# Half a turn later: low halves, value evictions and the norms of queries and keys in a two-block transformer kernel

## The chip, the cores and the metric

The kernel runs on one core of a Trainium2 chip. The metric is the device time of one execution in microseconds (us). Engines: PE is TensorE (matmuls; PEld its weight loads), DVE is VectorE, ACT is ScalarE, POOL is GpSimd, SP issues DMAs. Each engine works through its own queue in order and waits on semaphores of the others.

## The reference, cut to what matters

A sequence of 512 tokens with 1024 features goes through a first block and then two layers of a second one, all in float32. The first block has MoBA attention (8 heads of 64, queries and keys normed by head, a T5 bias), gated linear attention and a feed-forward part. Each of the two later layers has FoX attention (8 heads of 64, causal, a forget bias), retention (4 heads of 128) and a feed-forward part.

```python
mq = rms_norm(mq.reshape(B, S, MOBA_HEADS, MOBA_HEAD_DIM), moba_q_norm_g[layer])
mk = rms_norm(mk.reshape(B, S, MOBA_HEADS, MOBA_HEAD_DIM), moba_k_norm_g[layer])
...
p = softmax(q @ k.T * scale + bias)   # per head, causal
out = p @ v
```

The first two lines are the reference's; the last two sum up what both attentions compute (with 512 keys, MoBA's selected blocks are all past ones).

## The kernel before, in words

**Products.** Activations lie transposed (features on partitions, 512 tokens in a row). Every float32 product is made of three fp32r matmuls, high x high, high x low and low x high (`product`, L263 to L271); the same with the roles changed is `gemm_tok` (L335 to L340). So each operand needs a high half (a copy on ACT) and a low half (a subtraction on DVE). `prepare` (L239, L240) makes them for a weight piece of 128x1024, three pieces ahead; `piece` calls it at the start of a product of eight `product` steps. A product's PSUM bank (banks 0 to 3 in turn) is evicted by a function that is given to `gemm`: to `val` for MoBA's queries and keys (L712), to `gqk` (L521), and for FoX's rotary tiles by four DVE operations (L1346 to L1353).

**Ticks.** After each `product` the program calls `tick()`. A tick runs what `after_ticks(n, f)` has due, and then, by `pace[0]` steps per tick, steps of the background generator. This all happens when the instructions are issued to the queues: it fixes the order in each engine's queue, not a time. The attention heads are such a generator, `softmax_heads`, at 0.42 steps per tick in MoBA and 0.46 in FoX. A tick is some 0.69 us of PE work.

**Heads.** The generator goes through 32 turns (8 heads of 4 query blocks). Turn n has two steps. The first queues the reciprocal of turn n+2 (DVE, L635), the normalising of turn n+1 (ACT, L640), the scores of turn n+3 (PE, L616 and L618) and their bias, maximum and copy to SBUF (DVE, L621). The second queues, when n is a multiple of four, the weighing of the head that is complete (`weigh`, PE, L662, eight matmuls into bank 7) with its eviction, then the Exp of turn n+3 (ACT, L630), the transposes of turn n (PE, L647, into bank 6), and their high half (ACT, L652) and low half (DVE, L653). The transposes of the next turn wait until both halves have read bank 6. The weighing waits for the halves of all four turns. The eviction (`both_halves`, L698 on ACT, L699 on DVE) adds the two halves of the value product; for odd FoX heads a `split` into the operand Q follows (L399 on ACT, L400 on DVE).

**Norms of MoBA's queries and keys.** The evicted tile `val` waits nine ticks; then `qk_norm` (L580 to L597) queues at once: Square (ACT, L584), the mean over each head as a matmul with the constant `blk` into bank 7 (PE, L585), Ln (L586) and Exp (L588) on ACT, the gain on DVE (L591), and the splits of `queries` (L556, L557) or `keys` (L571, L572, with two copies by DMA each on POOL's queue). There are eight tiles, m = 0 to 7. The first two are evicted together, so their norms are due at the same tick. `rms_scale` and the gated linear attention use tB and other banks of their own.

Of the kernel before, what the change touches and what calls it, by code (L numbers as in the profile page):

```python
# [7 lines left out]
F32 = mybir.dt.float32  # L8
# [3 lines left out]
ALU = mybir.AluOpType  # L12
ACT = mybir.ActivationFunctionType
# [80 lines left out]
def build(nc, xT, w_in, gate_up, w_bm, w_bg, w_out, w_up, w_down, w_in2, w_out2, w_ff1, w_ff2,  # L94
          consts, params, out, vrev, cneg):
    ctx = ExitStack()
    with ctx:
        base = -(-nc.sbuf_base // 64) * 64

        def at(name, off_kb, shape, dt=F32):  # L100
            return nc.alloc_sbuf_tensor_at(name, shape, dt, offset=base + int(off_kb * KB))

        def sem(name):
            return Sem(ctx.enter_context(nc.semaphore(name)))

        PE, V, A, G, SP = (Queue(sem(n)) for n in ("s_pe", "s_dve", "s_act", "s_pool", "s_sp"))
# [24 lines left out]
        ident, blk = cst[:, 0:128], cst[:, 128:256]  # L131
# [4 lines left out]
        banks = [ctx.enter_context(nc.psum_tensor(f"ps{i}", [128, 512], F32)) for i in range(8)]  # L136
        free = [None] * 8
# [224 lines left out]
        def after_ticks(n, f):  # L362
            pending.append([n, f])
# [72 lines left out]
        sq = [at("sq0", g0 + 80, [128, S]), at("sq1", g0 + 82, [128, S])]  # L436

        sq_free, rb_free = [None, None], [None]
# [16 lines left out]
        t_const = [c9, t_prm, t_cst]  # L455
# [24 lines left out]
        val = [at(f"val{i}", g0 + 14 + 2 * i, [128, S]) for i in range(2)]  # L480
# [97 lines left out]

        val_free = [None, None]

        def qk_norm(heads, m, t_in):

            j, v, s = m // 2, val[m % 2], sq[m % 2]
            t = A.op(lambda e: e.activation(s[:, :], v[:, :], ACT.Square), t_in, sq_free[m % 2])  # L584
            t = PE.op(lambda e: e.matmul(banks[7][:, :], blk, s[:, :], start=True, stop=True), t, free[7], t_const)  # L585
            t = A.op(lambda e: e.activation(tB[:, :], banks[7][:, :], ACT.Ln, bias=epsc), t, rb_free[0])  # L586
            free[7] = t
            t = A.op(lambda e: e.activation(s[:, :], tB[:, :], ACT.Exp, scale=-0.5), t)  # L588
            rb_free[0] = t
            gain = prm[:, V_MK:V_MK + 1] if m % 2 else mqs  # L590
            t = V.op(lambda e: e.scalar_tensor_tensor(out=v[:, :], in0=v[:, :], scalar=gain, in1=s[:, :],  # L591
                                                      op0=ALU.mult, op1=ALU.mult), t)
            sq_free[m % 2] = t
            if m % 2:
                val_free[1] = heads.keys(j, v, t, t_xread)
            else:
                val_free[0] = heads.queries(j, v, t, 1.0, t_xread)  # L597

        def softmax_heads(heads, vv, t_v, bias_of, finished):

            t_max, t_exp, t_ri, t_pt, t_norm, biases = {}, {}, {}, {}, {}, {}
            hi_T, lo_T = PT

            def bias_for(n):
                if n < 32:
                    biases[n] = bias_of(n // 4, n % 4)

            def scores(n):
                if n >= 32:
                    return  # L610
                h, i = n // 4, n % 4
                w, sb, p, c = 128 * (i + 1), 4 + n % 2, pS[n % len(pS)], n
                bias, t_b = biases[n]
                qs, kh, kl = heads.tiles(h)
                q = qs[:, 128 * i:128 * i + 128]
                PE.op(lambda e: e.matmul(banks[sb][:, 0:w], q, kh[:, 0:w], start=True, stop=False),  # L616
                      heads.t[h], free[sb], signal=False)
                t = PE.op(lambda e: e.matmul(banks[sb][:, 0:w], q, kl[:, 0:w], start=False, stop=True))  # L618
                if n % 8 == 7:
                    heads.last_score[n // 8] = t  # L620
                t = V.op(lambda e: e.tensor_tensor_reduce(p[:, 0:w], banks[sb][:, 0:w], bias, -1.0, 3.0e38,  # L621
                                                          ALU.add, ALU.min, nm[:, c:c + 1]), t, t_b, pS_free[n % len(pS)])
                free[sb] = bias_read[n % 2] = bias_done[n] = t
                t_max[n] = t

            def exponentials(n):
                if n >= 32:
                    return
                w, p, c = 128 * (n % 4 + 1), pS[n % len(pS)], n
                t_exp[n] = A.op(lambda e: e.activation(p[:, 0:w], p[:, 0:w], ACT.Exp, bias=nm[:, c:c + 1], scale=-1.0,  # L630
                                                       accum_out=sm[:, c:c + 1]), t_max[n])

            def reciprocals(n):
                if 0 <= n < 32:
                    t_ri[n] = V.op(lambda e: e.reciprocal(ri[:, n:n + 1], sm[:, n:n + 1]), t_exp[n])  # L635

            def normalise(n):
                if 0 <= n < 32:
                    w, p = 128 * (n % 4 + 1), pS[n % len(pS)]
                    t_norm[n] = A.op(lambda e: e.activation(p[:, 0:w], p[:, 0:w], ACT.Copy, scale=ri[:, n:n + 1]), t_ri[n])  # L640

            def turn(n):
                h, i = n // 4, n % 4
                w, p = 128 * (i + 1), pS[n % len(pS)]
                t = t_norm[n]
                for j in range(i + 1):
                    t2 = PE.op(lambda e, j=j: e.transpose(banks[6][:, 128 * j:128 * j + 128],  # L647
                                                          p[:, 128 * j:128 * j + 128], ident), t, free[6])
                pS_free[n % len(pS)] = t2
                hi, lo = (x[:, i:4 * i + 1:3, :] for x in (hi_T, lo_T))  # L650
                src = banks[6][:, 0:w].rearrange("p (j q) -> p j q", j=i + 1)
                t = A.op(lambda e: e.activation(hi, src, ACT.Copy), t2, PT_free[0])  # L652
                t2 = V.op(lambda e: e.tensor_tensor(lo, src, hi.bitcast(F32), ALU.subtract), t, t2)  # L653
                free[6] = [t, t2]
                t_pt.setdefault(h, []).append([t, t2])

            def weigh(h):
                o = banks[7][:, :]
                for j in range(4):
                    for x in (hi_T, lo_T):  # L660
                        last = j == 3 and x is lo_T
                        t = PE.op(lambda e, j=j, x=x, last=last: e.matmul(  # L662
                            o[:, 128 * j:S], vv[:, j, h, :], x[:, 4 * j:3 * j + 4, :].rearrange("p b c -> p (b c)"),
                            start=(j == 0 and x is hi_T), stop=last), t_pt[h], t_v, free[7], signal=last)
                PT_free[0] = t
                free[7] = finished(h, o, t)

            bias_for(0)
            bias_for(1)
            for n in range(-3, 32):  # L670
                while not heads.ready((n + 3) // 4):
                    yield
                reciprocals(n + 2)
                normalise(n + 1)
                scores(n + 3)
                bias_for(n + 5)
                yield
                if n >= 4 and n % 4 == 0:
                    weigh(n // 4 - 1)
                exponentials(n + 3)  # L680
                if n >= 0:
                    turn(n)
                yield
            yield
            weigh(7)

        def split_values(vv, b, o, t, sc, *waits):

            o8 = o.rearrange("p (h d) -> p h d", h=8)
            hi, lo = vv[:, b, :, 0:64], vv[:, b, :, 64:128]  # L690
            t1 = A.op(lambda e: e.activation(hi, o8, ACT.Copy, scale=sc), t, list(waits))
            t2 = V.op(lambda e: e.scalar_tensor_tensor(out=lo, in0=o8, scalar=sc, in1=hi.bitcast(F32),
                                                       op0=ALU.mult, op1=ALU.subtract), t1, t)
            return [t1, t2]
# [6 lines left out]
        pS_free, PT_free = [None] * 4, [None]  # L701
# [6 lines left out]
        moba = Heads(ring)  # L708

        def ev_val(m):  # L710
            def ev(o, t):
                t1 = V.op(lambda e: e.tensor_tensor(val[m % 2][:, :], o, rB[:, :], ALU.mult),  # L712
                          t, t_rB, t_xread, val_free[m % 2])
                after_ticks(9, lambda: qk_norm(moba, m, t1))
                return t1
            return ev

# [47 lines left out]
        t = gemm_thin(P, glow[:, :], None)  # L765
# [195 lines left out]
        for j in range(8):  # L961
# [5 lines left out]
            s = sq[j % 2]  # L967
# [282 lines left out]
        for L in range(2):  # L1250
# [27 lines left out]
            t1 = V.op(lambda e: e.memset(one8, 1.0), t_ph)  # L1278
            t_c = V.op(lambda e: e.tensor_tensor_scan(cs[:, :], one8, lsg, 0.0, ALU.mult, ALU.add), t1, box[0])
            t1 = V.op(lambda e: e.tensor_scalar(lsb, cs[:, :], -1.0, None, ALU.mult), t_c)  # L1280
# [278 lines left out]
```

How the kernel before makes its waits and increments, by code:

```python
    def run(self, eng):  # L85
        for need, fn, s, inc in self.ops:
            for w, v in need:
                eng.wait_ge(w.h, v)
            ins = fn(eng)
            if s:
                ins.then_inc(s.h, inc)
# [1400 lines left out]
        @block.sync  # L1492
        def _(e):
            SP.run(e)
            e.wait_ge(s_out.h, s_out.n)
```

## Time and profile before

| | us |
|---|---|
| median of 3 runs | 2193.93 (2193.04 to 2195.63) |
| the profiled execution | 2193.07 |
| its span | 2191.1 |
| PE busy | 2089.3 |
| PE's mean granted clock | 0.986 |

The span is what the trace covers, from the first to the last instruction. Busy is the time in which an engine had work under way; the ends of matmuls are modelled. The granted clock is a share of the full rate of TensorE. In lines of the timeline the first number is the start in us from the span's start, the second the duration; what stands in brackets is the idle time of the engine before the line, and what ended it. A wait for several semaphores is put down to the one that came last by the profile.

### The profile page before, as it was taken

The page shows a single profiled execution, that of the slowest core. Times are in us where ns is not written, and L with a number is a line of the kernel's source. Part 1 is how long each engine was busy: PE and PEld are TensorE (multiplying, and loading weights), DVE is VectorE, ACT ScalarE, POOL GpSimd, SP SyncE. Part 2 cuts the span into 40 slices and gives each one's busy share as a digit, 9 for nine tenths or more (in the row PEclk, how much of TensorE's full clock was granted, in tenths as well). Part 3 has the DMA queues.
Part 4 walks back from the last instruction along what each step waited for, and adds up shares of the span by engine and source line. Part 5 has one row for each costly group of instructions (what it writes and reads, how often), then busy time and mean ns, then how long its engine had stood idle before and what let it go on. Part 6 is the DMA issues. An engine that isn't in the chain of part 4 may idle for free.

```text
span 2191.1 us, 24398 instructions
## 1 busy us (share of the span) xinstructions
PE 2089.3 (95%) x9592; PEld 1702.0 (78%) x9592; DVE 1120.9 (51%) x1744; ACT 924.7 (42%) x1497; POOL 189.8 (9%) x258
## 2 busy tenths in 40 slices
PE   6999999999999999999998999998999998999997
PEld 5778767888888888777787888887777677888886
DVE  4555554655433434567466333337667465333336
ACT  4565222524422323455546243343565346243343
POOL 0000000000000000243011000002353010000001
PEclk9999999999999999999999999999999999999998
DMA  6332211323223232633221223232533231323231
GB/s 210 87 92 74 77 58 58 135 92 101 96 95 98 96 96 78 183 92 97 101 96 59 96 96 96 96 96 59 164 106 92 92 96 58 96 96 96 96 96 58
DMA packets 201517, 211.36 MB, mean 96 GB/s; under 512 B 7803, under 2 KB 181115, under 8 KB 201404
## 3 DMA queue, kind: packets, MB, share of 16 engines
q1 hardware_dynamic: 194544, 194.13, 27.8%
q0 software_dynamic: 6352, 15.24, 2.7%
q8 instruction: 76, 1.25, 0.2%
q10 hardware_dynamic: 508, 0.43, 0.1%
q14 instruction: 37, 0.30, 0.0%
HBM read 194.55 MB, written 8.95 MB: 93 GB/s over the span
## 4 chain that ended last, share of the span: by engine, by line
PE 82%; DVE 8%; ACT 7%; issue 2%; DMA 0%; POOL 0%; DVEq 0%; ACTq 0%; SPq 0%
PE ps L267 23%; PE ps L270 23%; PE ps L269 23%; PE ps L335 2%; PE ps L340 2%; PE ps L338 2%; PE ps L662 1%; PE ps L647 1%; ACT H L1119 1%; PE ps L1412 1%; DVE wl L240 1%; ACT wh L239 1%; PE ps L1398 1%; ACT Phi L1122 1%; DVE d L1066 1%
## 5 line engine op out<-in xcount | busy, mean ns | idle before, releaser
L267 PE MATMUL ps<-Phi,wh 128*128 128x512 f32 (+1 forms) x1520 | 610.5, 402 | 37.3 <-DVE Plo L1123 20.4
L270 PE MATMUL ps<-Phi,wl 128*128 128x512 f32 (+1 forms) x1520 | 587.6, 387 | 0.0
L269 PE MATMUL ps<-Plo,wh 128*128 128x512 f32 (+1 forms) x1520 | 587.4, 386 | 0.0
L239 ACT ACTIVATE wh<-stage 128x1024 fp32r<-128x1024 f32 (+1 forms) x339 | 351.6, 1043 | 289.8 <-PE ps L270 278.7
L240 DVE TENSOR_TENSOR wl<-stage,wh 128x1024 fp32r<-128x1024 f32 x333 | 406.4, 1222 | 70.3 <-ACT wh L239 62.9
L267 PE MATMUL ps<-Qhi,wh 128*128 128x512 f32 (+1 forms) x1056 | 402.7, 381 | 0.8 <-DVE Qlo L400 0.8
L270 PE MATMUL ps<-Qhi,wl 128*128 128x512 f32 (+1 forms) x1056 | 399.2, 378 | 0.0
L269 PE MATMUL ps<-Qlo,wh 128*128 128x512 f32 (+1 forms) x1056 | 399.2, 378 | 0.0
L267 PEld LDWEIGHTS ps<-Phi,wh 128*128 128x128 f32 x1520 | 290.5, 191 | 104.5 <-issue 43.7
L270 PEld LDWEIGHTS ps<-Phi,wl 128*128 128x128 f32 x1520 | 290.0, 191 | 58.0
L269 PEld LDWEIGHTS ps<-Plo,wh 128*128 128x128 f32 x1520 | 290.9, 191 | 53.6 <-issue 4.1
L267 PEld LDWEIGHTS ps<-Qhi,wh 128*128 128x128 f32 x1056 | 200.9, 190 | 38.8 <-ACT Qhi L399 1.6
L269 PEld LDWEIGHTS ps<-Qlo,wh 128*128 128x128 f32 x1056 | 200.8, 190 | 37.4 <-issue 1.0
L270 PEld LDWEIGHTS ps<-Qhi,wl 128*128 128x128 f32 x1056 | 200.7, 190 | 36.4
L400 DVE TENSOR_TENSOR Qlo<-f,Qhi 128x512 fp32r<-128x512 f32 x96 | 66.5, 693 | 253.3 <-ACT Qhi L399 253.3
L1009 DVE TENSOR_TENSOR H<-H,ps 128x512 f32<-128x512 f32 x74 | 50.8, 687 | 221.1 <-PE ps L270 221.1
L985 ACT ACTIVATE rl<-ps 128x512 f32<-128x512 f32 x64 | 38.2, 598 | 194.7 <-PE ps L270 194.7
L990 ACT ACTIVATE f<-rl 128x512 f32<-128x512 f32 x96 | 60.7, 632 | 116.6 <-DVE rl L987 114.5
L335 PE MATMUL ps<-wh,Phi 128*128 128x512 f32 x224 | 92.5, 413 | 1.9 <-DVE x_rb L1351 1.9
L340 PE MATMUL ps<-wl,Phi 128*128 128x512 f32 x224 | 89.1, 398 | 0.0
L338 PE MATMUL ps<-wh,Plo 128*128 128x512 f32 x224 | 88.8, 396 | 0.0
L1310 POOL TENSOR_SCALAR x_bi<-x_Cb,stat 128x128 f32<-128x128 f32 (+1 forms) x64 | 69.3, 1083 | 116.1 <-DVE stat L621 110.1
(287 smaller groups left out, 1899.9 us busy)
## 6 DMA issues: line engine op xcount, KB each, us to landing
stage<-in_w_ff SPq DMA_DIRECT2D x64, 1024.0 KB, 5.3
stage<-in_w_in SPq DMA_DIRECT2D x39, 1024.0 KB, 5.1
stage<-in_w_up SPq DMA_DIRECT2D x16, 1024.0 KB, 5.2
stage<-in_w_down SPq DMA_DIRECT2D x16, 1024.0 KB, 5.2
stage<-in_w_in SPq DMA_DIRECT2D x30, 512.0 KB, 5.0
stage<-in_w_out SPq DMA_DIRECT2D x12, 1024.0 KB, 5.3
stage<-in_w_bg SPq DMA_DIRECT2D x4, 1024.0 KB, 5.5
vrev<-H SPq DMA_DIRECT2D x2, 2048.0 KB, 12.6
```

Of the source, the lines that this page charges most:

```text
L239: t_hi = A.op(lambda e: e.activation(hi, src, ACT.Copy), st_landed[n], w_free[i % 4], sem=s_whi)
L240: t_lo = low.op(lambda e: e.tensor_tensor(lo, src, hi.bitcast(F32), ALU.subtract), st_landed[n], t_hi, w_free[i % 4], sem=s_wlo if low is ...
L267: PE.op(lambda e: e.matmul(o, hi[:, k, c], x.hi[:, kx, tok], start=first, stop=False), t_hi, t_x or x.t[kx], list(waits), signal=False)
L269: PE.op(lambda e: e.matmul(o, hi[:, k, c], x.lo[:, kx, tok], start=False, stop=False), signal=False)
L270: return PE.op(lambda e: e.matmul(o, lo[:, k, c], x.hi[:, kx, tok], start=False, stop=last), t_lo, sem=s_wpe, signal=last)
L335: PE.op(lambda e, k=k, kk=kk, sl=sl, o=o, hi=hi: e.matmul(o, x.hi[:, kk, sl], hi[:, k, :], start=(kk == 0), stop=False), t_hi, x.t[kk], fr ...
L338: PE.op(lambda e, k=k, kk=kk, sl=sl, o=o, hi=hi: e.matmul(o, x.lo[:, kk, sl], hi[:, k, :], start=False, stop=False), signal=False)
L340: t = PE.op(lambda e, k=k, kk=kk, sl=sl, o=o, lo=lo: e.matmul(o, x.hi[:, kk, sl], lo[:, k, :], start=False, stop=(kk == 7)), t_lo, sem=s_w ...
L400: t2 = V.op(lambda e: e.tensor_tensor(lo, src, hi.bitcast(F32), ALU.subtract), t1, t_src, x.free, after)
L990: t = A.op(lambda e: e.activation(f[:, :], r[:, :], ACT.Square), t_r, f_free[j % 2])
L1009: t_h[j] = V.op(lambda e: e.tensor_tensor(H[:, j, :], H[:, j, :], o, ALU.add), t, t_h[j])
L1310: t = G.op(lambda e: e.tensor_scalar(bi[n % 2][:, 0:w], Cb[h % 2][:, 0:w], stat[:, 96 + 8 * i + h:97 + 8 * i + h], None, ALU.add), t_Cb[h] ...
```

## The change

A list `owed` of closures and `settle()`, which queues all of them in order, are added. `qk_norm` becomes three stages: `qk_square` at tick 2 after the eviction queues the Square, `qk_mean` at tick 9 calls `settle()` and queues the matmul, and `qk_scale` (Ln, Exp, gain, splits) is put on the list, which is settled two ticks later or by the generator, whichever comes first. In `turn` the low half is put on the list, and in `weigh` the eviction. The generator settles in the first step of a turn behind the reciprocal and the normalising and ahead of the scores, and at the start of the second step. It has one step more at its end.

```diff
+        owed = []
+
+        def settle():
+            while owed:
+                owed.pop(0)()
+
+        def qk_square(heads, m, t_in):
+
+            v, s = val[m % 2], sq[m % 2]
+            t = A.op(lambda e: e.activation(s[:, :], v[:, :], ACT.Square), t_in, sq_free[m % 2])
+            after_ticks(7, lambda: qk_mean(heads, m, t))
+
+        def qk_mean(heads, m, t):
+
+            settle()
+            s = sq[m % 2]
+            t = PE.op(lambda e: e.matmul(banks[7][:, :], blk, s[:, :], start=True, stop=True), t, free[7], t_const)
+            sq_free[m % 2] = free[7] = t
+            owed.append(lambda: qk_scale(heads, m, t))
+            after_ticks(2, settle)
+
+        def qk_scale(heads, m, t):
...
-            t = A.op(lambda e: e.activation(s[:, :], v[:, :], ACT.Square), t_in, sq_free[m % 2])
-            t = PE.op(lambda e: e.matmul(banks[7][:, :], blk, s[:, :], start=True, stop=True), t, free[7], t_const)
...
-                t2 = V.op(lambda e: e.tensor_tensor(lo, src, hi.bitcast(F32), ALU.subtract), t, t2)
-                free[6] = [t, t2]
-                t_pt.setdefault(h, []).append([t, t2])
+
+                def low():
+                    t3 = V.op(lambda e: e.tensor_tensor(lo, src, hi.bitcast(F32), ALU.subtract), t, t2)
+                    free[6] = [t, t3]
+                    t_pt.setdefault(h, []).append([t, t3])
+                owed.append(low)
...
-                PT_free[0] = t
-                free[7] = finished(h, o, t)
+                PT_free[0] = free[7] = t
+
+                def end():
+                    free[7] = finished(h, o, t)
+                owed.append(end)
...
                 reciprocals(n + 2)
                 normalise(n + 1)
+                settle()
                 scores(n + 3)
                 bias_for(n + 5)
                 yield
+                settle()
                 if n >= 4 and n % 4 == 0:
                     weigh(n // 4 - 1)
                 exponentials(n + 3)
                 if n >= 0:
                     turn(n)
                 yield
+            settle()
             yield
             weigh(7)
+            yield
+            settle()
...
-                after_ticks(9, lambda: qk_norm(moba, m, t1))
+                after_ticks(2, lambda: qk_square(moba, m, t1))
```

## Rows read from the trace of the kernel before

**Rows 1.** The page, busy us of each engine (share of the span).

```profile
PE 2089.3 (95%) x9592; PEld 1702.0 (78%) x9592; DVE 1120.9 (51%) x1744; ACT 924.7 (42%) x1497; POOL 189.8 (9%) x258
```

**Rows 2.** Windows: stretch, length, busy us by engine, granted clock, DMA share, GB/s.

```profile
64.00:232.00 168.00, 159.20 (x748) 127.62 (x748) 89.91 (x201) 92.72 (x190) 9.64 (x18) 0.99 0.28 82
905.00:1060.00 155.00, 148.12 (x718) 120.47 (x717) 103.77 (x221) 84.84 (x178) 61.05 (x85) 1.00 0.35 100
1560.00:1716.00 156.00, 146.05 (x706) 118.82 (x704) 101.52 (x220) 83.68 (x177) 61.94 (x84) 1.00 0.37 105
...
44.40:49.10 4.70, 4.67 (x12) 3.41 (x13) 1.54 (x3) 2.61 (x5) 0.96 (x3) 0.64 0.37 116
...
160.50:165.30 4.80, 4.80 (x14) 3.56 (x14) 2.28 (x4) 2.77 (x5) 0.53 (x1) 0.64 0.01 3
...
1716.60:1722.00 5.40, 5.40 (x16) 3.77 (x17) 1.02 (x3) 0.00 (x0) 0.00 (x0) 0.68 0.93 361
```

**Rows 3.** Waits: PE in MoBA, twice FoX (first, second layer), then DVE's.

```profile
PE ps L585 <- ACT sq L584: 6.4, 4, 2.5
...
PE ps L647 <- DVE stat L635: 2.6, 4, 0.9
PE ps L647 <- ACT tB L640: 2.0, 2, 1.6
...
PE ps L647 <- DVE stat L635: 3.0, 3, 1.2
...
PE ps L647 <- ACT tB L640: 2.1, 2, 1.2
...
DVE x_PT L653 <- ACT x_PT L652: 47.3, 49, 2.7
```

**Rows 4.** Timeline of PE: two means in MoBA, a matmul after FoX.

```profile
44.43 0.70 PE L585 MATMUL ps<-sq,cst 128*128 128x512 f32 x1 [4.19 <-ACT sq L584]
...
85.11 0.70 PE L585 MATMUL ps<-sq,cst 128*128 128x512 f32 x1 [1.33 <-ACT sq L584]
...
1716.59 0.48 PE L1398 MATMUL ps<-x_rqk 128*128 128x256 f32 x1 [2.17 <-DVE x_IT L1401]
```

**Rows 5.** Timeline of ACT between the first two means.

```profile
40.28 0.69 ACT L586 ACTIVATE tB<-ps,rcol 128x512 f32<-128x512 f32 x1 [8.96 <-PE ps L585]
...
43.75 0.63 ACT L584 ACTIVATE sq<-val 128x512 f32<-128x512 f32 x1
```

**Rows 6.** Timeline of DVE around turn 19 of the first FoX layer.

```profile
1004.72 0.69 DVE L653 TENSOR_TENSOR x_PT<-ps,x_PT 128x512 fp32r<-128x512 f32 x1 [1.26 <-ACT x_PT L652]
1005.33 0.68 DVE L1346 SCALAR_TENSOR_TENSOR x_rqk<-ps,x_tab 128x512 f32<-128x512 f32 x1
...
1009.23 0.16 DVE L635 RECIPROCAL stat<-stat 128x1 f32<-128x1 f32 x1
```

**Rows 7.** Timeline of PE there: the next product, and the weighing.

```profile
1004.92 0.39 PE L267 MATMUL ps<-Phi,wh 128*128 128x512 f32 x1
...
1007.41 0.61 PE L662 MATMUL ps<-x_PT,x_fvv 128*128 128x512 f32 x2
```

**Rows 8.** The first and last of 15 places: reciprocal and next transposes.

```profile
931.46 0.15 DVE L635 RECIPROCAL stat<-stat 128x1 f32<-128x1 f32 x1
...
931.15 0.39 PE L647 MATMUL ps<-cst,rB 128*128 128x128 f32 x2
...
1686.40 0.15 DVE L635 RECIPROCAL stat<-stat 128x1 f32<-128x1 f32 x1
...
1686.19 0.38 PE L647 MATMUL ps<-cst,rB 128*128 128x128 f32 x2
```

**Rows 9.** Timeline of ACT: eviction and split of an odd FoX head.

```profile
956.18 0.59 ACT L698 ACTIVATE x_yf<-ps 64x512 f32<-64x512 f32 x1 [3.38 <-PE ps L662]
957.52 0.63 ACT L399 ACTIVATE Qhi<-x_yf 128x512 fp32r<-128x512 f32 x1 [0.75 <-DVE x_yf L699]
```

More of the change, by code:

```diff
@@ L579, in build @@
         val_free = [None, None]
-        def qk_norm(heads, m, t_in):
+        owed = []
[14 more added lines that the diff above has]
+        def qk_scale(heads, m, t):
             j, v, s = m // 2, val[m % 2], sq[m % 2]
-            t = A.op(lambda e: e.activation(s[:, :], v[:, :], ACT.Square), t_in, sq_free[m % 2])
-            t = PE.op(lambda e: e.matmul(banks[7][:, :], blk, s[:, :], start=True, stop=True), t, free[7], t_const)
             t = A.op(lambda e: e.activation(tB[:, :], banks[7][:, :], ACT.Ln, bias=epsc), t, rb_free[0])
```

## The prediction

> **What bounds the kernel now.** The page first: TensorE (PE) is busy 95% of the span, DVE 51%, ACT 42% [rows 1]. Time moves only when PE's idle time or its clock does. The change touches three stretches: MoBA's heads beside the first projections, and the two FoX layers' heads beside theirs. The windows give PE 159.2 of 168 us in the first, 148.1 of 155 and 146.1 of 156 in the others [rows 2]: 29 us of idle time in all, all that a perfect overlap could win there. Then the waits by stretch: in MoBA PE waits for the Square of the query and key norms (L584), 6.4 us in four waits after 64 us, and 4.19 us once before [rows 3, 4]. In the FoX layers the waits are those of transposes (L647), put down to the reciprocal and the normalising; 2.6 and 2.0 us in one layer, 3.0 and 2.1 in the other [rows 3]. PE does not read the reciprocals: the transposes wait for bank 6, which the low half (L653) frees, and the reciprocal is its neighbour in DVE's queue. So I read these as waits for low halves. Last, the clock: after the 4.19 us wait it was granted at 0.64 for 4.7 us, after the 2.5 us one too, and after 2.17 us at 1716.6 at 0.68 for 5.4 us [rows 2, 4]; after the 1.6 us one of the first FoX layer it stayed whole, as all of that stretch [rows 2, 3].
>
> **The norms in three stages.** Before, Square, the mean (PE), Ln, Exp, the gain (DVE) and the splits of one tile are queued at one tick, nine after its eviction. The mean stays at tick 9; Square goes to tick 2, the rest at most two ticks (1.4 us) behind the mean. Of eight means five wait now. The worst is the second: its Square stands on ACT behind Ln, Exp and two query splits of the first tile [rows 5], hence 4.19 us. After, both Squares are long done, but the second mean needs bank 7, which the first tile's Ln frees: mean end 40.25, Ln 40.28 to 40.97, so a wait of 0.8 remains. Saved: 3.4 us, and the 0.36 x 4.7 = 1.7 us of clock that followed [rows 2, 4]. Three more wait 1.3 us each, as at 85.11 [rows 4], only for a Square behind a weight piece: 4.0 us saved. The eighth (2.5 us [rows 3]) follows the fourth weighing by one tick. Its Square is early now, but `qk_mean` calls `settle()`, which only then queues the copy and the add that free bank 7, behind an Exp, a high half and a weight piece. It waits as long as before, by my count of the queue 0.4 us longer, and its clock loss stays. Bounds for it: 0 (all 2.5 and 1.7 saved) and 2 us more. Readiness of heads is no matter: in the order of issue no head is waited for, before or after. Norms: -9.1 + 0.4 = -8.7.
>
> **The low halves.** low(n) leaves the second half of turn n for the first half of turn n+1, behind that half's reciprocal. No work is added; DVE's order changes. What came between, the eviction of a finished product and the low part of the next weight piece, now goes ahead of it. Who waits: the transposes of turn n+1 (bank 6), or, for every fourth, the weighing. They come half a turn after the new place, some 1.7 us, where they were a whole turn away. The trace shows the new time itself: the same work is permuted, so low(n) ends about where the next reciprocal ends now. Take turn 19 of the first FoX layer [rows 6]: low 1004.72, then the four rotary operations from 1005.33 and the weight piece, reciprocal at 1009.23, ended 1009.38. The weighing that needs this low started at 1007.41 with no wait [rows 7]. After, it waits 2.0 us. I did this for all turns. It is late in 7 of the first FoX layer (0.5, 3.1, 1.7, 3.0, 2.0, 2.0, 2.6) and in 8 of the second (1.6, 1.3, 1.3, 3.0, 0.7, 3.1, 2.3, 0.4), 28.6 us together; the first and the last of the 15 are [rows 8]. In MoBA 1.9 us of DVE work comes between (0.68 and 1.22) instead of 4.0, and there it is late about once: +1, bounds 0 and 3.
>
> Against it stands what DVE gets back: it idled before 49 FoX lows, waiting for the high half, 47.3 us [rows 3]. What stood behind can start in that idle time, but not before its own product ends. In [rows 6] the idle is 1.26, but PE went on to its next product at 1004.92 [rows 7], 0.4 before the rotary operation began. Between these two I take 0.4, since nearly all of these cases are evictions that follow their product's end as closely: 15 x 0.4 = 6. With 1.26 everywhere the 28.6 would be about 12. Further, of the 9.7 us of waits at L647 now [rows 3] those that already follow such a place within a turn (about two thirds) come from DVE being behind, and the new wait lets it catch up: 6.4 us vanish; bounds 3 and 9.7.
>
> **The value products' evictions.** The copy, the add and, for odd FoX heads, the split (0.6, 0.7, 0.6, 0.7 us, two engines in turn [rows 9]) leave the head of ACT's queue, so Exp and the high half go first. That frees ACT, whose idle time costs nothing here. But the whole chain now stands ahead of low(4h+4). For even heads it is done in time. For the six odd heads inside the stretches the chain ends some 4.5 us after the weighing, the next transposes come 3.4 after: a wait of about 1, as they have today with the chain ahead of Exp. Net +1, bounds -3 and +5. The last head's eviction goes one step later: in one layer behind the last product, beside a load that lasts anyway: 0.
>
> **Sum.** MoBA -8.7 + 1 = -7.7. FoX 28.6 - 6 - 6.4 + 1 = +17.2. Together +9.5 on the profiled execution's 2193.07 us (span 2191.1), which lies 0.9 under the median 2193.93; on the median 2203.4. With all bounds at one end it would be some -6, at the other +24.
>
> **Rivals.** (a) Faster. DVE's idle time ahead of the lows pays for everything: evictions start so early that no low is late by more than its cover, and odd heads lose their wait. Place: DVE between turn n and the first half of n+1; it decides where a product ends more than the listed lateness before its eviction starts now. Then FoX gives -3 instead of +17, MoBA -8.7: 2182. For it: 47 us of idle time. Against: the rotary operations start right at their product's end, and are 2.8 us with 1.2 behind them. (b) No change. The lows are late, by half of what I count, since each wait makes the next unnecessary: FoX +8, total 0: 2194. (c) Slower still. A dozen waits of 2 to 3.5 us, and the clock falls after each third: 4 x 1.7 on top, 2210. The rows speak both ways (2.17 us dropped it, 1.55 not). The Trainium skill has a rule for it (TensorE: Matmul & The Clock Gate, A second HAM failure mode: psum-queue depth-cycling): frequent short idles between groups of matmuls make the clock swing between half and full rate. If it held for every new wait, it would be 13 x 1.7 = 22 us on top; the trace agrees only for the long ones. (d) The change does less than it says, since queues run ahead of each other anyway; for the Squares this is excluded, their order on ACT is what PE waits for [rows 5].
>
> **Numbers.** Forecast 0.57; (a) 0.17, (b) and (d) together 0.16, (c) 0.10. A measurement tells this kernel from no change at about 0.2%, 4.4 us. Faster is (a), 0.17; within 0.2% is (b), 0.16; slower is the forecast and (c), 0.67. Time 2203.4; its own range 2197 to 2210. For 8 in 10 the range takes in (b) and (c) and leaves out most of (a): 2190 to 2215.
>
> **What would show it.** Right: no wait of L585 over 1 us but one of 2 to 3 near 160; the window after 44 us at a whole clock; PE idle in 64 to 232 down by about 3 us; PE idle in the FoX stretches up from 7 and 10 to some 15 and 18, in waits of 2 to 3.5 us at transposes or weighings, each with a low half just ended and rotary operations and a weight piece ahead of it. Wrong: FoX stretches with as much PE work as before, or waits there under 1 us; or the eighth mean without a wait.

## The result, and the profile after

The changed kernel took 2218.49 us (median of 4 executions, 2213.47 to 2222.84) against 2194.53 for the kernel before (4 executions, 2193.04 to 2195.63). The ratio is 1.0109, 95% interval 1.0091 to 1.0128: 24 us slower. The forecast was 2203.4 with a range that ended at 2215. The sign was right; the size was not. In the experiments below medians are over all executions and the intervals over the undisturbed ones alone: one of e5_fox_at_once and two of the kernel before took 4036 to 7382 us, which moves a median by 0.24 us at most.

The four executions don't agree as those of before do, and the clock goes with them: mean granted clock 0.985 at 2213.47, 0.983 at 2214.97, 0.978 at 2222.01 and 2222.84. The profiled one is the longest of them, so a second profile of the same kernel (`e8_repeat`, 2213.96 us, clock 0.985, inside the forecast's range) is read beside it.

The page, busy us of each engine, stands against [rows 1]. PE has 15.8 us more to show for the same work:

```profile
PE 2105.1 (95%) x9592; PEld 1712.5 (77%) x9592; DVE 1124.2 (51%) x1744; ACT 928.7 (42%) x1497; POOL 191.2 (9%) x258
```

The same instructions take longer where the clock is lower: a full product 0.42 us in place of 0.23 (last section). So the time that came is of two kinds, idle time and clock, and each needs a ledger by stretch. The stretches are cut at the same two PE instructions in each kernel: the first transpose of the forget sums (`x_cs`) and the first product of `x_rqk` with itself, of each FoX layer. Before they stand at 906.0, 1078.5, 1557.9 and 1734.8 us. The columns are the change of each stretch against the kernel before, in us, by single profiles:

| profile | to the first FoX stretch (MoBA in it) | first FoX | between | second FoX | rest | all |
|---|---|---|---|---|---|---|
| changed, 2222.84 | -4.9 | +17.0 | 0.0 | +17.7 | +0.1 | +29.9 |
| changed again, 2213.96 | -8.7 | +16.0 | 0.0 | +13.8 | 0.0 | +21.0 |

All of it lies where the change is. Within a FoX stretch three numbers give the length: the idle time of PE before its instructions (timeline), the clock lost (windows of 5 us, each 5 x (1 - granted clock), added up), and what is left, which is the work.

| FoX stretch | length | idle | clock lost | left |
|---|---|---|---|---|
| before, first | 172.5 | 8.3 | 0.0 | 164.2 |
| before, second | 176.9 | 10.4 | 1.7 | 164.8 |
| changed (2222.84), first | 189.5 | 18.5 | 6.9 | 164.2 |
| changed (2222.84), second | 194.6 | 19.7 | 10.3 | 164.6 |
| changed (2213.96), first | 188.4 | 18.4 | 5.1 | 164.9 |
| changed (2213.96), second | 190.7 | 21.1 | 3.4 | 166.2 |

The work is the same to 2 us in all six rows. The change brought 19.5 us of idle time and 15.5 us of clock in the first profile, 20.8 and 6.8 in the second, where the work is 2.1 us more besides.

The windows of the kernel before over its two FoX stretches, rounded to whole us (columns as in [rows 2]):

```profile
906.00:1078.00 172.00, 163.75 (x778) 131.36 (x779) 109.97 (x231) 92.18 (x188) 61.05 (x85) 1.00 0.37 112
1558.00:1735.00 177.00, 166.46 (x784) 133.49 (x785) 108.75 (x230) 88.78 (x185) 62.48 (x85) 0.99 0.39 115
```

The same of the changed kernel; MoBA first, and last two places of 15 and 10 us that are read below:

```profile
28.00:232.00 204.00, 194.28 (x874) 153.25 (x874) 107.36 (x222) 107.36 (x209) 13.86 (x25) 0.97 0.35 102
901.00:1091.00 190.00, 171.31 (x781) 135.84 (x782) 111.29 (x232) 94.67 (x189) 61.21 (x85) 0.96 0.35 102
1570.00:1764.00 194.00, 174.28 (x782) 138.58 (x782) 109.92 (x230) 89.68 (x184) 63.58 (x85) 0.95 0.36 104
...
150.00:165.00 15.00, 12.34 (x44) 9.03 (x43) 7.68 (x17) 8.83 (x17) 2.08 (x4) 0.77 0.25 54
...
1670.00:1680.00 10.00, 7.16 (x24) 5.86 (x25) 4.24 (x13) 3.82 (x10) 3.28 (x4) 0.66 0.14 30
```

The DMA share is lower, DVE and ACT did the same work: neither became a bound. Who is waited for is in the waits of PE. Line numbers have moved: the mean is L597, the transposes L666, the weighing L684, the low half L674. MoBA (28 to 232 us):

```profile
PE ps L597 <- DVE ym L729: 2.7, 1, 2.7
...
PE ps L666 <- DVE PT L674: 1.5, 2, 0.9
...
PE ps L597 <- ACT tB L605: 0.8, 1, 0.8
```

First FoX stretch, then the second:

```profile
PE ps L666 <- DVE x_PT L674: 11.4, 9, 3.9
PE ps L684 <- DVE x_PT L674: 3.7, 3, 2.3
...
PE ps L666 <- DVE x_PT L674: 12.0, 9, 3.4
PE ps L684 <- DVE x_PT L674: 4.7, 4, 2.3
PE ps L635 <- DMA f0kl<-f0kl: 1.4, 1, 1.4
```

In [rows 3] the releaser of the transposes was the reciprocal or the normalising, neighbours of the low half. Now the low half itself is named, 25 times, for 31.8 us. The timeline of PE in the changed kernel, at the two means and at three places of FoX, to be read beside [rows 4] and [rows 7]:

```profile
41.82 1.12 PE L597 MATMUL ps<-sq,cst 128*128 128x512 f32 x2 [0.78 <-ACT tB L605]
...
153.43 1.22 PE L597 MATMUL ps<-sq,cst 128*128 128x512 f32 x1 [2.66 <-DVE ym L729]
...
959.67 0.66 PE L666 MATMUL ps<-cst,x_pS 128*128 128x128 f32 x2 [3.90 <-DVE x_PT L674]
...
1012.04 0.47 PE L684 MATMUL ps<-x_PT,x_fvv 128*128 128x512 f32 x1 [2.34 <-DVE x_PT L674]
...
1672.84 0.66 PE L666 MATMUL ps<-cst,x_pS 128*128 128x128 f32 x2 [3.36 <-DVE x_PT L674]
```

The fourth line is turn 19, the example of the prediction ([rows 6, 7]). DVE around it:

```profile
1007.24 0.69 DVE L1376 SCALAR_TENSOR_TENSOR x_rqk<-ps,x_tab 128x512 f32<-128x512 f32 x1 [1.72 <-PE ps L270]
...
1010.01 1.22 DVE L240 TENSOR_TENSOR wl<-stage,wh 128x1024 fp32r<-128x1024 f32 x1
1011.15 0.16 DVE L654 RECIPROCAL stat<-stat 128x1 f32<-128x1 f32 x1
1011.22 0.67 DVE L674 TENSOR_TENSOR x_PT<-ps,x_PT 128x512 fp32r<-128x512 f32 x1
```

The low half ends at 1011.9, the weighing starts at 1012.04. DVE stood idle for 1.72 us ahead of the rotary operations, waiting for their product: it had finished all that stood ahead of them, and the low half stands behind them in its queue.

### The profile page after: what moved, and what is told of

Same layout as the page of the kernel before. It is cut to its first block, busy times and chain, and to the rows that moved or that the text cites. A ratio compares the mean times of both kernels' runs of the same rounds, so it can differ in the third digit from the quotient of the medians.

```text
span 2221.0 us, 24367 instructions
## 1 busy us (share of the span) xinstructions
PE 2105.1 (95%) x9592; PEld 1712.5 (77%) x9592; DVE 1124.2 (51%) x1744; ACT 928.7 (42%) x1497; POOL 191.2 (9%) x258
## 3 DMA queue, kind: packets, MB, share of 16 engines
q1 hardware_dynamic: 194544, 194.13, 27.8%
q8 instruction: 76, 1.25, 0.2%
## 4 chain that ended last, share of the span: by engine, by line
PE 81%; DVE 9%; ACT 6%; issue 3%; DMA 1%; POOL 0%; DVEq 0%; ACTq 0%; SPq 0%
PE ps L267 23%; PE ps L270 22%; PE ps L269 22%; PE ps L335 2%; PE ps L340 2%; PE ps L338 2%; PE ps L666 1%; PE ps L684 1%; DVE wl L240 1%; ACT wh L239 1%; ACT H L1149 1%; PE ps L1442 1%; ACT Phi L1152 1%; PE ps L1428 1%; DVE d L1096 1%
```

## The experiments

Ten kernels. Each is the changed kernel with the edit shown, unless it says otherwise. Times are medians; the kernel before was measured beside them, at 2196.23 us for the first four, 2194.41 for the next four, 2194.84 for the last two.

| kernel | norms | low halves | value evictions | median us | against before, 95% interval |
|---|---|---|---|---|---|
| e1_norms | three stages | at once | at once | 2181.60 | 0.9939, 0.9925 to 0.9953 |
| e2_low | one | late | at once | 2241.68 | 1.0213, 1.0199 to 1.0226 |
| e3_end | one, with `settle()` | at once | late | 2199.94 | 1.0021, 1.0012 to 1.0030 |
| e4_settle_first | three | late, ahead of evictions | late, the same | 2191.95 | 0.9981, 0.9972 to 0.9990 |
| e5_fox_at_once | three | late in MoBA only | late | 2194.10 | 0.9996, 0.9988 to 1.0005 |
| e6_half_dose | three | late in MoBA, in FoX for odd turns | late | 2199.69 | 1.0029, 1.0017 to 1.0040 |
| e7_low_settle | one, with `settle()` | late | at once | 2228.89 | 1.0154, 1.0141 to 1.0167 |
| e8_repeat | three | late | late | 2216.88 | 1.0101, 1.0088 to 1.0114 |
| e9_one_end | three | at once | one per FoX layer late | 2189.73 | 0.9974, 0.9963 to 0.9985 |
| e10_norms_low | three | late | at once | 2218.08 | 1.0108, 1.0093 to 1.0124 |

And the ledger of their profiles, in the columns of the first one (e8 stands there), with the clock lost over the whole span (30.0 before, 49.3 in the changed kernel's first profile, 33.9 in its second). Clock lost outside the FoX stretches need not be time lost: the stretch between them takes the same time in all of them, with 8.5 to 13.7 us of clock lost in it.

| profile | to first FoX | first FoX | between | second FoX | rest | all | clock lost |
|---|---|---|---|---|---|---|---|
| e1_norms | -10.4 | +0.1 | +0.1 | -1.2 | 0.0 | -11.4 | 27.2 |
| e2_low | +12.0 | +19.0 | 0.0 | +21.8 | 0.0 | +52.9 | 52.3 |
| e3_end | -0.3 | +6.7 | 0.0 | +0.4 | 0.0 | +6.8 | 38.9 |
| e4_settle_first | -10.6 | +6.0 | +0.1 | +5.9 | 0.0 | +1.5 | 38.9 |
| e5_fox_at_once | -7.4 | +6.8 | 0.0 | +1.2 | 0.0 | +0.6 | 33.6 |
| e6_half_dose | -7.8 | +8.3 | 0.0 | +5.9 | 0.0 | +6.4 | 33.3 |
| e7_low_settle | +1.3 | +13.0 | 0.0 | +21.9 | 0.0 | +36.2 | 41.9 |
| e9_one_end | -11.7 | +3.2 | +0.1 | +1.8 | +0.4 | -6.2 | 29.1 |
| e10_norms_low | -9.5 | +13.5 | 0.0 | +16.8 | +0.2 | +21.0 | 32.7 |

### The norms alone

```diff
-                owed.append(low)
+                low()
...
-                owed.append(end)
+                end()
```

> Only the norms in three stages; low halves and value evictions are queued at once, as before. My theory (low halves behind evictions cost FoX its time, the norms gain): 3.4 + 4.0 us of waits at the means go, 1.9 of the eighth (its bank is freed early again) and 1.7 us of clock after the second mean, perhaps 1.7 after the eighth: 9 to 13 us faster than before, and in the FoX stretches waits and clock of before (6.6 and 6.2 us of waits). Rival (the gain of the norms is given back elsewhere, since PE only arrives earlier at other waits): within 4 us of before.

Measured: 14.6 us under the kernel before by medians, above the 9 to 13 expected, 11.4 by profiles, nearly all of it before the first FoX stretch. The rival is out. Its waits of PE in MoBA (28 to 225 us):

```profile
PE ps L597 <- ACT tB L605: 0.8, 1, 0.8
PE ps L597 <- DVE ym L729: 0.6, 1, 0.6
```

Before, this engine waited 10.6 us for Squares in this stretch. The eighth mean waits 0.6 us here and 2.7 in the changed kernel: that wait is made by the fourth head's eviction being owed, as the prediction said (in e10, where only the evictions are put back, it is 0.6 us too). This kernel is the fastest of all and beats both.

### The low halves alone

The kernel before, with `owed`, `settle()` and its calls in the generator, and the low half on the list; `qk_norm` in one piece, the eviction at once.

```diff
-            after_ticks(7, lambda: qk_mean(heads, m, t))
-
-        def qk_mean(heads, m, t):
-
-            settle()
...
-                owed.append(end)
+                end()
```

> Only the low halves queued half a turn later; norms and value evictions as before. My theory: all of FoX's new waits are here, 14 to 20 us of them, each at transposes or a weighing whose low half just ended, and the clock falls after those over 2 us, 5 to 14 us more: 17 to 33 us slower than before. Rival (the chain of copy, add and split ahead of the low half does it): under 8 us slower, since that chain stands ahead of Exp again.

Measured: +45 us by medians, beyond the 17 to 33 expected. The FoX stretches are longer by 19.0 and 21.8 us, and MoBA too, by 12, where I had put 1. Waits of PE there, and in the first FoX stretch (here the transposes are L653, the weighing L671, the low half L661):

```profile
PE ps L653 <- DVE PT L661: 10.7, 8, 3.2
...
PE ps L653 <- DVE x_PT L661: 12.6, 8, 4.0
PE ps L671 <- DVE x_PT L661: 3.7, 3, 2.3
```

In MoBA PE did not wait for a low half by name before. What stands ahead of it now is not the weight piece alone but the norm's gain and the low halves of the queries or keys (0.75 and 1.4 us on DVE, each after a wait for ACT). MoBA has no rotation: what my expectation for e7 calls so is these splits. e7 takes them away.

### The value evictions alone

```diff
-                owed.append(low)
+                low()
```

The norms are in one piece, with `settle()` at their head.

> Only the value products' evictions half a turn later; norms and low halves at once. My theory: low halves go ahead of the chain, so nobody waits for it but bank 7: within 5 us of before, rather faster, since Exp and the high half no longer stand behind it and the waits at odd FoX heads (0.8 to 1.9 us at six places) go: -3. Rival (the chain does it): 8 us or more slower.

Measured: 0.21% slower, 3.7 us by medians, inside the 5 but not the -3 expected; 6.8 by profiles, all of it in the first FoX stretch, where PE's idle time rose from 8.3 to 11.1 us and the clock lost from 0 to 5.1. The waits of PE there that stand out (L1416 and L1419 are the first matmuls of retention and their decay mask):

```profile
PE ps L335 <- DVE x_rb L1369: 3.7, 1, 3.7
...
PE ps L1416 <- DVE x_IT L1419: 2.2, 1, 2.2
```

Of the clock 3.4 us were lost after the first, at 1033 (e9 tests it), and 1.7 after the second, at 1067. Before, that second wait was 1.52 us and nothing was lost: the last head's eviction, with its idle times, now stands two operations nearer to the mask in DVE's queue. In the second FoX layer the same step makes it shorter, 0.9 us for 2.17, which is a good part of why a wait of 3.72 us there leaves the stretch only 0.4 us longer.

### Owed work ahead of each eviction

```diff
                     if q == 3:
+                        settle()
                         free[b] = evac(b, banks[b][:, :], t)
```

The same in `gemm`; `owed` and `settle` are defined further up.

> The changed kernel, but settle() is also called ahead of every product's eviction, so that no rotary operation, split or weight piece gets ahead of an owed low half. My theory: the waits of 1.5 us and more behind rotary operations go (some 12 of 33 us in FoX, with those behind key and query splits 18), those behind the chain of odd heads remain in part; the clock falls less often: within 6 us of the kernel before, at least 14 us faster than the changed one. Rival (half a turn is too short whatever stands ahead): still over 12 us slower than before.

Measured: 2191.95 us, 26 us under the changed kernel's 2218.49, with the owed work placed ahead of the evictions (the value evictions and the norms' last stage are on the same list and move with the low halves). Its waits of PE for low halves (transposes L668, weighing L686, low half L676) in the first FoX stretch, against 11.4 and 3.7 in the changed kernel:

```profile
PE ps L668 <- DVE x_PT L676: 6.3, 6, 2.6
...
PE ps L686 <- DVE x_PT L676: 0.6, 2, 0.4
```

So what stands ahead of the owed work makes most of the loss; e5, which moves nothing but low halves, shows that it is they. e4 still loses 10 us to e1. How much of that is the low halves' and how much the value evictions', no run separates; the half turn gains nothing even where it is cheap.

### FoX's low halves at once

```diff
-                owed.append(low)
+                if heads is not moba:
+                    low()
+                else:
+                    owed.append(low)
```

> The changed kernel, but in the forgetting attention (FoX) each low half is queued straight behind its high half again; in MoBA it stays half a turn late, and the value evictions and the norms stay as changed. Theory (the cost is the low halves behind the rotary evictions of the two FoX stretches, as waits of TensorE and as clock after them): TensorE's waits in the two FoX stretches fall back from 18 and 20 us to 7 to 11 each, the clock loss there from 7 and 10 us to 0 to 5 each, and the time to about 2187 us (2182 to 2194): the 2181.6 of the norms alone, plus 4 for the value evictions, plus 1 to 2 for the low halves of MoBA. Rival (the low halves cost as much in MoBA, and the clock is lost across the program whatever FoX does): above 2200 us.

Measured: 2194.10 us. All of the loss against the kernel before is gone, 24 us, and no wait put down to a low half is left in the first FoX stretch. The number is 7 us above the 2187 expected and at the edge of its range: the value evictions cost more (+6.8 and +1.2 in the two stretches, the clock lost there 5.1 and 3.4) than the 4 that I had added for them, and before the first FoX stretch it is 3.0 us behind e1. The rival, above 2200, is out.

### Half the low halves of FoX

```diff
+                if heads is not moba and n % 2 == 0:
+                    low()
+                else:
+                    owed.append(low)
```

> The changed kernel, but in FoX only the low halves of odd turns are late (16 per block in place of 32, about half of the 15 cases behind a rotary eviction). If both waits and clock follow the number of long waits: waits of TensorE in the FoX stretches of 12 to 15 us each, a clock loss there of 2 to 6 us each, and 2200 to 2206 us. Rival 1 (the clock falls only where waits follow each other closely, as a threshold): waits as above, clock loss in the FoX stretches back to that of before (0 and 2 to 5 us), 2193 to 2199 us. Rival 2 (one long wait in a stretch is enough for the clock): clock loss as in the changed kernel, 2207 to 2212 us.

Measured: 2199.69 us, between the first case and rival 1. Idle time in the FoX stretches 14.2 and 15.0 us, inside what all three cases had; clock lost there 1.7 and 1.7, below the first case and nearer to rival 1. Against e5 it costs 5.6 us for half the late halves, and the other half costs 17 more. The dose is not linear in the number of late halves: the waits of 3.9, 2.75 and 3.36 us belong to even turns and are not here, and after its four waits of 2.0 to 2.3 us for low halves no clock was lost. I take from it that length, not number, sets the price, but with the clock varying by several us between executions this one run does not settle it: the changed kernel's first profile lost 1.7 us after three waits of that length (2.03, 2.34 and 2.32).

### The low halves alone, with the list emptied at the norm

```diff
         def qk_norm(heads, m, t_in):
 
+            settle()
             j, v, s = m // 2, val[m % 2], sq[m % 2]
```

The base is e2_low.

> The kernel in which the low halves alone are late (norms in one stage, value evictions at once; 2241.7 us), with the queue of owed work emptied at the head of the norm of a query or key, as the changed kernel does ahead of its mean. Theory (part of the 46 us came from low halves that queued on VectorE behind the norm's products and the rotation in MoBA, which the changed kernel avoids): TensorE's waits in MoBA fall from 22 to 15 to 18 us, and the time to 2226 to 2236 us. Rival (that part of the wait is the norm's own, in one stage, and the low halves add nothing to it): MoBA's waits and the time stay, 2238 to 2245 us.

Measured: 2228.89 us, 11 to 13 under e2 (against the kernel before, or directly), inside the range expected. By profiles it is 16.7 us: 10.7 before the first FoX stretch (+12.0 becomes +1.3) and 6.0 within it, where the idle time is 18.9 us in both and the clock lost 8.5 us in e2 and 1.7 here. The second part is the clock's chance and not the edit's. Waits of PE for low halves at MoBA's transposes, 10.7 us in e2:

```profile
PE ps L654 <- DVE PT L662: 2.3, 3, 1.1
```

So `qk_mean`'s call of `settle()`, which costs the changed kernel 2.1 us at the eighth mean, should save it some 11 in MoBA by keeping low halves ahead of the norm's DVE work; with the norms in three stages no run tests it.

### The changed kernel once more

> The changed kernel once more, beside its variants. Theory: 2213 to 2223 us; where the executions differ by more than 2 us, the granted clock goes with the time (0.985 by 2213, 0.978 by 2222), since the same waits meet the throttle in another phase. Rival: the time moves by several us at an unchanged clock, so the spread lies in the transfers.

Measured: 2213.96 to 2218.35 us, clocks 0.985, 0.981, 0.981, 0.982. The waits are those of the first profile to 0.01 us at most places, the clock is not. The clearest pair is the wait of 3.36 us before the transposes in the second FoX layer, at 1672.84 in the first profile (clock 0.66 over the 10 us shown above) and at 1667.83 here:

```profile
1665.00:1675.00 10.00, 7.17 (x36) 6.03 (x36) 6.81 (x16) 4.55 (x11) 3.73 (x4) 1.00 0.14 30
```

The same at the eighth mean, 2.66 us in both: after it 0.77 over 15 us in the first, and here

```profile
150.00:165.00 15.00, 12.44 (x60) 9.97 (x60) 8.71 (x20) 8.95 (x20) 2.07 (x4) 1.00 0.34 85
```

The same wait cost the clock in one execution and not in the other. Over its four executions the clock goes with the time only roughly (0.981 at 2216.43, 0.982 at 2218.35).

### One value eviction late

```diff
-                owed.append(low)
+                low()
...
+                if heads is not moba and h == 5:
+                    owed.append(end)
+                else:
+                    end()
```

> The norms in three stages and every low half at once (2181.6 us), and of the value evictions one alone late: that of the sixth head (h == 5) of each FoX block, whose add and low half come on VectorE just ahead of a rotary eviction. Theory (a late value eviction costs by its place: at this one VectorE stands still for ScalarE's copy and high half, 0.76 and 0.70 us, and TensorE's next product waits 3.7 us in place of 1.1, after which the clock falls): both waits of 3.7 us appear, nothing else changes, and the time rises by 2 x 2.6 of wait and 2 to 5 of clock, to 2189 us (2187 to 2192), about as much as all eight late evictions of each block cost (7 us in the first FoX stretch, 1 to 2 in the second). Rival (the cost is spread over the eight): 2182 to 2185 us.

Measured: 2189.73 us, 8.1 above e1, for two evictions out of 24; in the FoX stretches of the profiles 3.1 and 3.0 us. Both waits are there, 3.66 and 3.72 us. In e1 the same product waits 1.10 and 0.73 and the transposes just before it 0.90 and 1.25, which are gone here, so that the idle time grew by 1.6 and 1.8 us a stretch and not by 2.6; the clock lost grew by 1.7 in each. The first on the timeline of PE:

```profile
1020.93 0.79 PE L335 MATMUL ps<-wh,Phi 128*128 128x512 f32 x1 [3.66 <-DVE x_rb L1384]
```

and what DVE did ahead of it:

```profile
1016.55 0.69 DVE L732 TENSOR_TENSOR x_yf<-ps,x_yf 64x512 f32<-64x512 f32 x1 [0.76 <-ACT x_yf L731]
1017.93 0.69 DVE L400 TENSOR_TENSOR Qlo<-x_yf,Qhi 128x512 fp32r<-128x512 f32 x1 [0.70 <-ACT Qhi L399]
...
1020.19 0.69 DVE L1384 SCALAR_TENSOR_TENSOR x_rb<-ps,x_tab 64x512 f32<-64x512 f32 x1
```

DVE stands still for 0.76 us for ACT's copy and 0.70 for ACT's high half, and PE's next product needs the bank that the third rotary operation reads. So a late value eviction is priced by its place: at this one it costs about 3 us by profiles, half of it clock. Of the others e3 shows only the last head's, at the mask of retention.

### Norms and low halves, evictions at once

```diff
-                owed.append(end)
+                end()
```

> The changed kernel with its value evictions queued at once again: norms in three stages, low halves late. Theory 1 (the parts add: the late value evictions cost 8 us of the changed kernel's time, as they do when nothing else is late): 2207 to 2211 us. Theory 2 (with late low halves the two don't add: an eviction that is queued at once only moves the waits, since in the kernel with the low halves alone the FoX stretches grew by 35 to 41 us against 30 to 35 with both): 2214 to 2226 us, TensorE's waits in the FoX stretches 17 and 20 us as there.

Measured: 2218.08 us, theory 2. With late low halves the evictions can stand at either place: idle time in the FoX stretches is 18.9 and 22.0 us, no less than in the changed kernel (18.4 to 21.1), and the waits for low halves in the first are

```profile
PE ps L666 <- DVE x_PT L674: 12.6, 8, 3.9
PE ps L684 <- DVE x_PT L674: 3.7, 3, 2.3
```

The wait of e9 at the sixth head is 1.05 us in the changed kernel, I take it because PE has already been stopped by low halves before it.

## Why the prediction was right in sign and too small

**The norms** (-8.7 with MoBA's low halves at +1, -7.7). Waits of PE in MoBA went from 15.2 to 9.6 us, -5.6, where the steps gave -6.0 (3.4, 4.0, less 0.4 and 1). The second mean waits 0.78 us (0.8 forecast), the eighth 2.66 (2.5 to 2.9 forecast), the Squares no longer appear. Of the clock I had given 1.7 us back, and after the second mean it came back in both profiles. The stretch is -8.7 in the second profile but -4.9 in the first, where the clock lost 1.7 us more than before at each of two other waits: the eighth mean's, and one that the change doesn't touch, 2.16 us at 29 us. e1 gives -10.4 for the norms without the rest, where the forecast's -9.1 and the 1.9 us saved at the eighth mean would be -11.0.

**MoBA's low halves** (+1). Waits at transposes and weighings are 1.5, 1.3 and 1.1 us, the 1.3 still put down to the reciprocal, against 1.2, 1.0 and 0.2 before: +1.5, of which e1 has 1.0 without late low halves. So the forecast held, but because `qk_mean` settles the list, as far as e7 shows; alone they cost 12 (e2). The prediction saw that call only as a cost.

**FoX's waits** (+17.2). Measured +19.5 and +20.8. The mechanism is the one named. All 15 listed places wait in the changed kernel: 0.92, 3.90, 1.61, 0.70, 2.34, 2.26 and 1.18 us in the first layer, 2.03, 1.80, 0.66, 2.75, 1.28, 3.36, 2.32 and 0.69 in the second. That is 27.8 us where the list had 28.6. **So one term of the sum failed: the 6 us given back by DVE's idle time.** Only 0.8 came, over all places together. At turn 19 one sees why: what stood behind the low half has to wait for its own product. The wait is 2.34 us, not 2.0 less 0.4, and the rotary operations waited 1.72 us. The other places were not taken apart in this way. The other waits at transposes and weighings are 4.0 us, near the 9.7 - 6.4 + 1 forecast; PE's remaining waits took 1.4 us back in the first profile (a DMA's 1.41 us stands where 2.07 us of another stood, and the waits for retention's mask went from 1.52 and 2.17 to 2.17 and 0.95).

The two longest waits, 3.90 and 3.36 us, are the two places that were listed with 3.1. Ahead of these low halves stand no rotary operations but the key split and a weight piece, and then the value eviction:

```profile
954.15 1.41 DVE L572 TENSOR_TENSOR f0kl<-ps,f0kh 64x512 fp32r<-64x512 f32 x2 [3.72 <-ACT f0kh L571]
955.92 1.23 DVE L240 TENSOR_TENSOR wl<-stage,wh 128x1024 fp32r<-128x1024 f32 x1 [0.36 <-ACT wh L239]
```

With the evictions at once (e10) they are 3.94 and 3.95 us, so the late evictions did not make them. Within this change the evictions' +1 agrees with e10 to a few us (2218.08 against 2218.49 and 2216.88), though not for the reason given: e3 and e9 show that late on their own they cost 4 to 8.

**The step that failed most is the clock.** The sum had the clock's price for one wait removed (1.7 us) and none for the waits added; that price stood in rival (c), with a chance of 0.10. In the profile of 2222.84 us the length of the FoX stretches grew by 34.7 us: 17.2 forecast, 2.3 more of waits, 15.5 of clock, less 0.3 of rounding. With MoBA 2.8 above its forecast this is all of the 20.4 us between +9.5 and +29.9. In the profile of 2213.96 us, +21.0, the excess is 11.5: 6.8 of clock, 3.6 more of waits, 2.1 of work, less 1.0 in MoBA. So in a short execution the clock is the largest part but not the whole. Not every loss followed a low half either: 3.4 us in each profile followed other waits (2.17 us for retention's mask in both, a DMA's 1.41 in the first, 2.08 at a product in the second), against 1.7 before.

[Rows 2] already had three waits of 2.17 us or more that were each followed by a clock of 0.64 to 0.68, and the forecast listed eight of 2 us or more in FoX. Two to three waits near 3 us per layer should have been priced in the sum, not in a rival. The trace of before also had a wait that spoke the other way and is not among the rows, 2.07 us at 1575.6, with the clock whole for the 10 us after it:

```profile
PE ps L267 <- ACT rB L630: 2.1, 1, 2.1
```

The rule of the Trainium skill (TensorE: Matmul & The Clock Gate, A second HAM failure mode: psum-queue depth-cycling) spoke for this side: it reports a kernel in which short idles between groups of matmuls make the clock swing. The runs agree with it in kind; the 22 us that the prediction works out with it, for every new wait at 1.7, are above what they show, 6.8 to 15.5.

**The rivals.** (a) is out: FoX's waits had to fall by 3 us and rose by 19.5, since what stands behind the low half is itself waiting. (b), half the count, is out by the waits. (c) had the mechanism, and its 2210 was closer than the forecast, but still low. (d) is out by e1.

**Two sums of the prediction do not come out.** The idle time of PE in its three windows is 25.6 us, not 29; nothing rests on it. And with all the bounds that it states at one end it gives -14.0 and +26.5, not -6 and +24.

## What to carry to other kernels

When an operation is moved behind others in an in-order queue, the lateness can be read off the trace of before with good accuracy: the permuted order keeps its times, and the 15 places came out at 27.8 us for 28.6. What the moving engine's idle time would give back has to be checked at each place against the end of the product that comes next. And a wait of TensorE can cost more than its length. Price each new wait of over about 2 us with its wait and with the clock behind it, and give a kernel that gains such waits a wider range, since the same wait costs the clock in one execution and not in the next. And undo a change in parts: here one part gained 14.6 us, one lost more than that, and the third cost 4 us alone and nothing clear of noise beside the second.

## What the runs showed of the hardware

Over twelve profiles of this kernel and its variants, counted around the two FoX stretches (890 to 1080 and 1560 to 1760 us): the clock was lost (more than 1 us in the 5-us window in which the wait ended and the next together) after 2 of 86 waits of PE between 0.8 and 1.7 us, after 32 of 65 between 1.7 and 3 us, and after 16 of 17 of 3 us and more. The one exception is the 3.36 us wait of the repeat. Where it was lost, most often it was 1.7 us, or twice that, the latter where the clock stayed down longer. A full matmul of PE (128x128 by 128x512) takes 0.23 us from start to start at the whole clock and 0.42 at the lower of its two levels (1.2 against 2.4 GHz), which is why its busy time grows by as much. That a wait that is not changed at all sometimes has this price and sometimes not, I had not expected. Two profiles show it plainly: e2 and e7 have the same 18.9 us of idle time in the first FoX stretch and lost 8.5 and 1.7 us of clock. In the changed kernel's first four executions the clock goes with a spread of 9 us; the four of its repeat spread over 4.4, no more than the kernel before (3 to 5), so it is not shown that the change widened the spread. What decides the loss in an execution no run here shows.
